# A 128-byte shift of the activation buffers in SBUF: a two-block transformer on one NeuronCore

## The reference

```
# block 1
u = rmsnorm(x, norm_mix_w);  proj = u @ w_in + b_in          # 1024 x 5888
y_conv = (cb * causal_dwconv(cc * cx)) @ w_conv_out
y_attn = sliding_window_attention(rope(q), rope(k), v) @ w_attn_out + b_attn_out
x = x + (sigmoid(g_conv) * y_conv + sigmoid(g_attn) * y_attn) @ w_mix_out
up, gate = split(rmsnorm(x, norm_ffn_w) @ w_ffn_up)          # 1024 x 5632
x = x + (silu(causal_dwconv(up)) * gate) @ w_ffn_down        # 2816 x 1024
x = rmsnorm(x, norm_final_w)
# block 2
mod = silu(c) @ w_mod + b_mod                                # 1024 x 9216, nine shifts, scales, gates
x = x + gate1 * swiglu(modulate(rms_norm(x)), w1_gate, w1_up, w1_down)
x = x + gate2 * hybrid_mixer(modulate(rms_norm(x)))          # 8 stick-breaking heads, 8 forgetting heads
x = x + gate3 * swiglu(modulate(rms_norm(x)), w2_gate, w2_up, w2_down)
```

## Time and profile before

| | us |
|---|---|
| median of 3 runs | 1893.49 |
| lowest and highest of them | 1890.17, 1894.01 |
| profiled execution, its own time | 1890.17 |
| its span in the trace | 1888.4 |
| PE busy in that span | 1849.2 |
| DVE busy | 983.7 |
| ACT busy | 682.2 |
| POOL busy | 38.0 |

### The profile page before, as it was taken

The page is one execution under the profiler, slowest core; times in us unless marked ns, Lnnn a source line. Parts: engine busy times, 40 slices in busy tenths (PEclk is TensorE's granted clock), DMA queues, the critical chain, the costliest instruction groups (busy, mean ns, idle before and its releaser), DMA issues.

```text
span 1888.4 us, 20842 instructions
## 1 busy us (share of the span) xinstructions
PE 1849.2 (98%) x8613; PEld 1540.7 (82%) x8613; DVE 983.7 (52%) x1335; ACT 682.2 (36%) x1017; POOL 38.0 (2%) x72
## 2 busy tenths in 40 slices
PE   6899999999999999999999999999999999999998
PEld 5688888887888888888888888888888778888887
DVE  5555554457776766773333334657667453333332
ACT  5344442234332322353222223455566242222222
POOL 0000000000000000000000000101200000000001
PEclk9999999999999999979999999999999999999999
DMA  3222223354675665613333333222121223333333
GB/s 116 73 78 79 80 82 90 96 151 116 204 221 175 202 203 172 206 44 112 91 99 101 91 100 89 79 56 56 45 56 45 78 78 101 90 100 101 91 93 95
DMA packets 321716, 200.03 MB, mean 106 GB/s; under 512 B 6696, under 2 KB 311126, under 8 KB 321622
## 3 DMA queue, kind: packets, MB, share of 16 engines
q1 hardware_dynamic: 320128, 196.17, 35.8%
q0 software_dynamic: 640, 2.10, 0.4%
q10 hardware_dynamic: 854, 0.43, 0.1%
HBM read 196.57 MB, written 2.10 MB: 105 GB/s over the span
## 4 chain that ended last, share of the span: by engine, by line
PE 88%; DVE 4%; ACT 3%; DMA 3%; issue 1%; SPq 0%; POOL 0%; DVEq 0%; ACTq 0%
PE ps L1292 87%; DMA w_raw<-in_w_ffn_up 2%; PE ps L1295 1%; ACT w_hi L367 1%; DMA w_raw<-in_w_ffn_down 1%; DVE mod_acc L843 1%; DMA x_in<-in_x 0%; DVE t_b L814 0%; DVE w_lo L781 0%; DVE t_b L1019 0%; ACT t_b L403 0%; ACT y_hi L552 0%; DVE u_lo L802 0%; DVE x L825 0%; DVE ssum L792 0%
## 5 line engine op out<-in xcount | busy, mean ns | idle before, releaser
L1292 PE MATMUL ps<-u_hi,w_hi 128*128 128x512 f32 x1688 | 668.9, 396 | 9.0 <-DVE u_lo L802 3.3
L1292 PE MATMUL ps<-u_lo,w_hi 128*128 128x512 f32 x1688 | 661.0, 392 | 0.0
L1292 PE MATMUL ps<-u_hi,w_lo 128*128 128x512 f32 x1688 | 661.0, 392 | 0.0
L781 DVE TENSOR_TENSOR w_lo<-w_raw,w_hi 128x1024 fp32r<-128x1024 f32 (+2 forms) x307 | 364.4, 1188 | 286.6 <-ACT w_hi L367 285.9
L367 ACT ACTIVATE w_hi<-w_raw 128x1024 fp32r<-128x1024 f32 (+2 forms) x307 | 314.6, 1025 | 234.1 <-DMA w_raw<-in_w_down 76.9
L1292 PEld LDWEIGHTS ps<-u_hi,w_hi 128*128 128x128 f32 x1688 | 319.7, 189 | 81.0 <-issue 11.0
L1292 PEld LDWEIGHTS ps<-u_hi,w_lo 128*128 128x128 f32 x1688 | 319.2, 189 | 67.5
L1292 PEld LDWEIGHTS ps<-u_lo,w_hi 128*128 128x128 f32 x1688 | 319.6, 189 | 66.9 <-issue 2.4
L1292 PE MATMUL ps<-y_hi,w_hi 128*128 128x512 f32 x656 | 255.9, 390 | 1.1 <-DVE y_lo L1021 1.1
L1292 PE MATMUL ps<-y_hi,w_lo 128*128 128x512 f32 x656 | 255.3, 389 | 0.0
L1292 PE MATMUL ps<-y_lo,w_hi 128*128 128x512 f32 x656 | 255.3, 389 | 0.0
(11 more groups left out here) (255 smaller groups left out, 1427.3 us busy)
## 6 DMA issues: line engine op xcount, KB each, us to landing
mod_raw<-in_w_mod SPq DMA_DIRECT2D x72, 512.0 KB, 4.3
w_raw<-in_w_in SPq DMA_DIRECT2D x71, 512.0 KB, 3.8
w_raw<-in_w_ffn_up SPq DMA_DIRECT2D x44, 512.0 KB, 5.0
w_raw<-in_w_gate SPq DMA_DIRECT2D x44, 512.0 KB, 3.8
w_raw<-in_w_up SPq DMA_DIRECT2D x44, 512.0 KB, 3.8
w_raw<-in_w_down SPq DMA_DIRECT2D x32, 512.0 KB, 3.7
w_raw<-in_w_ffn_down SPq DMA_DIRECT2D x16, 512.0 KB, 5.7
w_raw<-in_w_down SPq DMA_DIRECT2D x16, 384.0 KB, 3.4
```

The source lines that it names most:

```text
L781: e.tensor_tensor(w_lo[u % SLOTS][:, 0:n_k, :], w_raw[u % SLOTS][:, 0:n_k, :], f32(w_hi[u % SLOTS][:, 0:n_k, :]), ALU.subtract).then_inc(l ...
L1292: return e.matmul(out_, lhsT, rhs, start=start, stop=stop, skip_group_check=skip)
```

## The change

The unused buffer becomes 16 values, 64 bytes, wide. No instruction is added, removed, resized or moved in any engine's order. What changes is the address in the instructions that touch a buffer written behind `align` in the code: `u_hi` begins at 89600, and it and all later buffers lie 128 bytes lower. Everything up to `t_b1`, the weights' buffers among them, stays.

```
         t_a = [sb(f"t_a{n}", [P, SEQ + 2]) for n in range(2)]
         t_b = [sb(f"t_b{n}", [P, SEQ]) for n in range(2)]

-        sb("align", [P, 48])
+        sb("align", [P, 16])
         u_hi = sb("u_hi", [P, KC, SEQ], F32R)
         u_lo = sb("u_lo", [P, KC, SEQ], F32R)
```

## The result

The change makes the kernel slower: 1925.86 us in the median of 4 runs (1925.47 to 1927.15) against 1891.83 before (the three runs of the kernel before and one more), a ratio of 1.0181 (95% interval 1.0164 to 1.0199). The profiled execution took 1925.6 us, with a span of 1923.1, 34.7 more than before. The forecast was no change; what came is rival B, and dearer than its price of 21 us.

The account below looks back on a forecast made before the run. The prediction took PE's rate of successive matmuls to bound the kernel; its terms, 0 + 0 + 0 - 0.4 us on the runs' median of 1893.49, gave 1893 us, with a range of 1887 to 1899.

Parts of the forecast that it names:

- rival B: PE's weight and activation streams, now 128 bytes apart, collide and slow each matmul: 21 us at 3 ns, 1914 us; chance 9%.
- What bounds the kernel: PE, busy 1849.2 of 1888.4 us: 7128 matmuls at 0.227 us, 86% of the span; faster loads win 2.3 us at most.
- The moving operand's start: PE's matmuls: moving operand's start modulo 256 taken to cost 0, bounded by 1 ns per matmul, at the far end 13 ns.
- The distance: PE's matmuls: 128 bytes between moving and stationary starts taken to cost 0, upper bound 3 ns each, 21 us.
- DVE, ACT, POOL: Their instructions on shifted buffers: taken at 0; 2 us for DVE and ACT with 1 ns on each of roughly 2300.
- DMA: Transfers of `x_in`, `mod_raw` and `out_sb`: a gain of 0 to 3.4 us, 0.4 taken.
- rival C: DMA transfers on moved buffers: pieces of 256 bytes matter and all 3.4 us of gain come, 1890 us; chance 8%.
- Rival A: PE's matmuls: the fixed 13 ns are a start penalty that vanishes at 0 modulo 256, gaining 95 us, 1798; chance 5%.
- The 13 ns: PE: the part of a 512-column matmul's 227 ns that doesn't grow with the columns, where an unfavourable start could hide.

Follow-up runs that it names:

- e1: Kernel before with an unused 128-byte buffer ahead of `w_hi0`, `align` kept at 48, so weights and activations both begin at 0 modulo 256: 1889.35 us, ratio 0.9995.
- e11_probe_widths: Kernel before plus added matmul groups ahead of the first unit: fp32r of 128 to 512 columns and bf16, at several distances: 2056.41 us.
- e9_probe: Kernel before plus some 900 matmuls on a separate buffer, ahead of the first unit, at distances of 0 to 240 bytes and with alternating starts: 2091.59 us.
- e5_low_weights_128: Kernel before with an unused 128-byte buffer ahead of `w_raw0`, `align` at 16: only `w_lo`, `w_raw` and `x` to `t_b1` lie 128 bytes higher: 1918.01 us.
- e8_align_56: Kernel before with `align` at 56 values instead of 48, a distance of +32 bytes: 1932.20 us.
- e2: Kernel before with an unused 128-byte buffer ahead of `w_hi0` and `align` at 16: weights' side 128 bytes higher, activations unmoved: 1927.04 us, ratio 1.0199.
- e6: Kernel before with `align` at 112 values instead of 48, a distance of +256 bytes: 1891.73 us.
- e3: Kernel before with `align` at 80 values instead of 48, a distance of +128 bytes: 1926.87 us.

## Why the prediction was wrong

**What bounds the kernel** was right: PE's rate over 7128 matmuls, with more than 0.53 ns of it outside the runs' scatter, and loads on the chain that were worth almost nothing.

**The moving operand's start**, taken at 0 from the earlier trace rows: right for the place (e1). But the comparison couldn't have shown rival B. `w_p` over `v` both begin at 128 modulo 256, `mask_win` over `ones_r` both at 160: distance 0 in both rows. And both have 256 columns, a width at which e11_probe_widths finds no loss at any distance it tried.

**The distance**, taken at 0 with a bound of 3 ns, is the step that failed. It rested on two things.
- "over eight tiles the two lie at many distances". They lie 512 k and 2048 k bytes in, so all those distances are multiples of 512. The period is 256 bytes: each of the 1035 matmuls of the earlier trace rows was at distance 0, the one place without a loss. A sample whose step is a multiple of the period says nothing about the period.
- `p` over `tri_neg`, the one pair of 512 columns off the beat, by -32 bytes. Its 0.230 us was read as 227 plus rounding. The probe's step at 224 bytes is 233.4. The row is given to 10 ns, over two steps: 0.46 us is 225 to 235 each. The bound had to be the row's upper end, 8 ns, and not its middle. Then rival B would have read 7128 x 8 = 57 us at its worst, and the forecast's certainty had no ground; the loss that came, 5.46 ns, lies inside. In nanoseconds the two steps are 231 and 229, alike at 1251, 1282, 1313 and 1344: the 3 ns were there and no rounding. And two matmuls say little of a long stream: the probe's first steps at 224 bytes are 227, 235, 231 and 229, and it settles at 231 to 235.

**DVE, ACT, POOL** at 0: right. L850, L851 and L814 stay at 751 to 752 ns, with their sums unchanged.

**DMA**, 0.4 of a possible 3.4 us of gain: no gain in time was seen, and rival C can't be told inside the loss. `x_in` took 8.20 us on the chain where the earlier trace rows had 8.59, but across the runs with the buffer at 128 modulo 256 it is 8.11 to 8.72, and with it at 0 it is 8.20 to 8.84: scatter. `mod_raw` lands after 4.3 us as in the earlier trace rows. The stores did gain, from 2.8 to 2.5 us:

```profile
mod_raw<-in_w_mod SPq DMA_DIRECT2D x72, 512.0 KB, 4.3
...
out<-out_sb POOLq DMA_DIRECT2D x8, 256.0 KB, 2.5
```

**Rival A** fell with e1. The 13 ns remain at either place. The argument against it from 128 columns rested on a single step: after the 0.06 us of the earlier trace rows the next matmul of that width, from 104.34, takes 0.11 us to the one below, and a stream of them takes 111.7 ns each in e11_probe_widths.

```profile
104.45 0.27 PE L1292 MATMUL ps<-w_p_hi,v_lo 128*128 128x128 f32 x1
```

bf16 at 215.9 ns is what the Trainium skill gives in "TensorE: Matmul & The Clock Gate", "Wait — 56ns, not 53.3ns?", N / 2.4 + 2.5, and the trace agrees; fp32r at its best distance pays 10.8 ns more. What those are is open, and they are worth 7128 x 10.8 = 77 us here.

**Rival B** had the mechanism in its first form, two reads of PE that disturb each other by their distance. Its price was the mis-sized term: 3 ns against 5.46, 21 us against the 34 measured. What counted against it, that each read passes over both halves many times, is not borne out by e9_probe: the starts settle into a cycle that stays the same from one matmul to the next, and the loss stays with it. That this is because the two reads keep their relation to the addresses is my reading and not shown.

**Still open** is which reads meet. e5_low_weights_128 and the alternating groups show that neither the tile in use nor the tile being loaded is the sole partner, 112 bytes held two different patterns, and a stream at distance 0 is slow for some steps behind another one.

## What to carry to other kernels

Where a kernel is bound by a dense stream of fp32r matmuls with 512 columns and a weight tile loaded beside each, put the moving and the stationary buffers at the same place modulo 256 bytes, and look it up in the built addresses whenever any buffer ahead of them changes size: a resized scratch buffer cost 1.8% here and up to 2.2% (e8_align_56). It is shown for places of 0 and 128 modulo 256. When a trace is asked whether an address matters, first work out which distances its rows really cover, and take a row's rounding as part of its bound. A tie between loads and matmuls shows as loads on the chain at almost no idle time of PE; they are worth only that idle time.

## What the runs showed that was not expected

- The start-to-start time of 512-column fp32r matmuls depends on the distance of the two operands' starts modulo 256 bytes: 226.7 ns at 0 once settled, 228.9 to 240.0 elsewhere, from 4 bytes on, without any other engine at work; 112 bytes gave 226.7 in one probe and 230.9 in the other. bf16: 215.9 at every distance.
- The loss isn't spread evenly but comes in cycles of starts, seven steps long at 128 bytes (228 to 241 ns), and two cycles can exist for one distance. After a change of distance it can take ten steps to reach the new one.
- Stores whose source starts at 0 modulo 256 were quicker. The packets of `out_sb`, 4096 bytes each in the trace, took 215 ns in the mean with the source at 128 modulo 256 (213 in e2, 215 in e6) and 158 at 0 (159 in e1, 158 in e3). Loads into `mod_raw` kept a median of 159 ns at either. The rule that the prediction took from the Trainium skill ("DMA: Bandwidth & Descriptors", "How a descriptor splits into AXI transactions") has the direction right on the side that reads SBUF, but not the size: its 132 beats against 128 are 3%, and the packets became 26% shorter. On the side that writes SBUF nothing is seen.
